# Every engine's work in another order: one table of dates replaced in a one-core kernel of three transformer blocks

## The reference

```python
hid = jnp.einsum('cd,ced->ce', xc, jnp.take(u, ec, axis=0))
w = gc * jax.nn.gelu(hid, approximate=False)
return jnp.einsum('ce,ced->cd', w, jnp.take(v, ec, axis=0))
```

## Time and profile before

| | us |
|---|---|
| median of three runs | 2318.24 |
| lowest and highest | 2311.13, 2322.93 |
| span of the profiled execution | 2204.1 |
| median less that span | 114.1 |

### The profile page before, as it was taken

One profiled execution on the slowest core, in us unless ns is written; L12 is line 12 of the kernel. 1 busy time (PEld: TensorE's weight loads), 2 busy tenths in 40 slices (PEclk: granted clock), 3 DMA queues, 4 the chain that ended last, 5 costly groups with the idle time before them and its releaser, 6 DMA issues.

```text
span 2204.1 us, 28240 instructions
## 1 busy us (share of the span) xinstructions
PE 1852.7 (84%) x10240; PEld 1223.7 (56%) x10240; DVE 1473.0 (67%) x3734; ACT 726.2 (33%) x1882; POOL 1124.4 (51%) x1028
## 2 busy tenths in 40 slices
PE   6999886689897687898677999877299988999998
PEld 3798575457544173545125565431166655567786
DVE  1388688855658776457896356587868778567564
ACT  3466123345422111321021153102025533346363
POOL 0000035575767676677776577676775667640000
PEclk8999897798898899999898999988689999999999
DMA  9999868799999999999999999999999999995360
GB/s 391 376 407 362 318 250 307 268 385 363 407 379 337 406 363 406 395 373 406 389 405 409 399 397 375 406 368 389 366 394 401 363 374 360 356 409 201 134 243 26
DMA packets 213459, 774.85 MB, mean 352 GB/s; under 512 B 23868, under 2 KB 24776, under 8 KB 213320
## 3 DMA queue, kind: packets, MB, share of 16 engines
q0 software_dynamic: 147456, 536.94, 63.5%
q1 hardware_dynamic: 65864, 236.11, 27.4%
HBM read 770.80 MB, written 2.16 MB: 351 GB/s over the span
## 4 chain that ended last, share of the span: by engine, by line
PE 39%; POOL 20%; DMA 18%; DVE 13%; issue 7%; ACT 2%; SPq 0%; DVEq 0%; ACTq 0%; POOLq 0%
POOL gat L1475 20%; PE ps L717 15%; DMA gat<-in_peer_v_dram,idxv 8%; DMA gat<-in_peer_u_dram,idx 7%; PE ps L1582 5%; DVE gat L1494 4%; PE ps L1235 3%; PE ps L1650 2%; PE ps L1013 2%; PE ps L1033 2%; PE ps L2723 1%; DVE ws L2108 1%; DVE ws L2106 1%; PE ps L821 1%; DMA wbuf<-in_win_dram 1%
## 5 line engine op out<-in xcount | busy, mean ns | idle before, releaser
L1494 DVE CUSTOM_DVE_ANT_0 gat<-gat,X 128x1024 f32<-128x1024 f32 x512 | 615.3, 1222 | 311.3 <-DMA gat<-in_peer_u_dram,idx 306.6
L1475 POOL DMA_INDIRECT gat<-in_peer_u_dram,idx x512 | 571.0, 1115 | 470.0 <-DVE ws L1327 292.2
L1475 POOL DMA_INDIRECT gat<-in_peer_v_dram,idxv x512 | 553.2, 1080 | 388.0 <-PE ps L1582 198.9
L717 PE MATMUL ps<-hn,wbuf 128*128 128x256 f32 (+1 forms) x2976 | 593.5, 357 | 38.6 <-DVE ws L1152 10.9
L717 PEld LDWEIGHTS ps<-hn,wbuf 128*128 128x128 f32 x2976 | 505.2, 197 | 124.6 <-issue 40.5
L1582 PE MATMUL ps<-gat,spread 128*32 128x512 f32 x2048 | 426.9, 656 | 113.0 <-DMA gat<-in_peer_v_dram,idxv 98.6
L1582 PEld LDWEIGHTS ps<-gat,spread 128*32 128x32 f32 x2048 | 81.8, 115 | 381.9 <-DMA gat<-in_peer_v_dram,idxv 227.8
L1235 PE MATMUL ps<-wbuf,oT 128*128 128x512 f32 x208 | 94.7, 609 | 2.7 <-DVE oT L1211 2.3
L1102 ACT ACTIVATE ws<-ws 128x16 f32<-128x16 f32 (+6 forms) x224 | 77.2, 347 | 35.0 <-DVE ws L1169 28.8
L861 DVE CUSTOM_DVE_ANT_0 gat<-gat,row 128x1024 f32<-128x1024 f32 x64 | 76.1, 1219 | 8.4 <-DMA gat<-in_ada_dram 4.3
L717 PE MATMUL ps<-ws,wbuf 128*128 128x256 f32 x256 | 61.9, 407 | 15.3 <-DVE ws L960 15.3
(11 more groups left out here) (373 smaller groups left out, 2599.1 us busy)
## 6 DMA issues: line engine op xcount, KB each, us to landing
wbuf<-in_win_dram SPq DMA_DIRECT2D x160, 512.0 KB, 8.3
gat<-in_ada_dram SPq DMA_DIRECT2D x120, 512.0 KB, 12.4
wbuf<-in_wout_dram SPq DMA_DIRECT2D x34, 512.0 KB, 6.5
wbuf<-in_pq_dram SPq DMA_DIRECT2D x32, 512.0 KB, 8.5
wbuf<-in_kvw_dram SPq DMA_DIRECT2D x32, 512.0 KB, 8.7
gat<-in_kvada_dram SPq DMA_DIRECT2D x16, 512.0 KB, 14.4
gat<-in_peer_u_dram,idx POOLq DMA_INDIRECT x512, 7.5
gat<-in_peer_v_dram,idxv POOLq DMA_INDIRECT x512, 7.8
```

The source lines that it names most:

```text
L717: i = e.do.matmul(psum, wview(name, g, kc // 2, turn)[:, kc % 2, m * P:m * P + P], src[:, kc, :], start=kc == 0, stop=kc == KC - 1)
L1475: e.do.indirect_dma_start(gat[g][:, :], None, t["peer_" + kind], bass.IndirectOffsetOnAxis(at, 0)).then_inc(*ldg[g].put(kind, l, b, *unit))
L1494: e.do.tensor_tensor_reduce(g[:, :], g[:, :], X[b % 2][:, :], 1.0, 0.0, ALU.mult, ALU.add, hid[:, e_ // 16 % 2, e_ % 16:e_ % 16 + 1]).then ...
```

## The change

The table `LATE` of corrections becomes a table `PLAN` of dates, now for all five engines, GpSimd too; where `PLAN` has a date, the base date no longer counts. The order in which weight tiles are loaded, and with it their slots, comes from a new list `LOADS`. No step has other instructions than before. Since waits are on semaphores' counts at the producer's place in its list, they move with the steps.

```diff
-def weave(late, *parts):
+def weave(at, *parts):
...
-        return t + late[n][step] if n < len(late) and step < len(late[n]) else t
+        return at[n][step] if n < len(at) and step < len(at[n]) else t
...
-    LATE = [
...
+    LOADS = [
+        ("win", 0, 0), ("win", 1, 0), ("win", 2, 0), ("win", 3, 0), ("win", 4, 0), ("win", 5, 0), ("win", 6, 0), ("win", 7, 0), ("wout", 0, 0),
...
+    PLAN = {
+        "PE": [
+            [6.57, 6.58, 11.07, 35.42, 38.1, 52.76, 53.2, 89.46, 93.11, 95.57, 104.82, 105.26, 118.16, 120.62, 129.86, 137.43],
...
-        loads.extend(sorted((when, key) for key, when in first.items()))
+        loads.extend(sorted(((when, key) for key, when in first.items()),
+                            key=lambda load: (LOADS.index((*load[1][:2], load[1][3])), load)))
...
-        weave(LATE_SP, *parts, sp_start(e), sp_ada(e), sp_weights(e), sp_kept(e), sp_sub(e), sp_bias(e), sp_store(e))
+        weave(PLAN["SP"], *parts, sp_start(e), sp_ada(e), sp_weights(e), sp_kept(e), sp_sub(e), sp_bias(e), sp_store(e))
...
-        weave([], *[pool_experts(e, l, c) for l in range(2) for c in range(2)])
+        weave(PLAN["POOL"], *[pool_experts(e, l, c) for l in range(2) for c in range(2)])
```

More of the change, by code:

```diff
@@ L446, in layer_stack_kernel @@
     T_FINISH = [1705.451, 1757.451, 1903.422, 2011.985]
-    LATE = [
-        [
[63 rows of a table removed]
-        ],
-        [
[68 rows of a table removed]
-        ],
-        [
[68 rows of a table removed]
-        ],
-        [
[3 rows of a table removed]
-        ],
-    ]
-    LATE_PE, LATE_ACT, LATE_DVE, LATE_SP = LATE
+    LOADS = [
+        ("win", 0, 0), ("win", 1, 0), ("win", 2, 0), ("win", 3, 0), ("win", 4, 0), ("win", 5, 0), ("win", 6, 0), ("win", 7, 0), ("wout", 0, 0),
+        ("wout", 1, 0), ("pq0", 0, 0), ("pq0", 1, 0), ("win", 1, 1), ("win", 0, 1), ("win", 2, 1), ("win", 3, 1), ("win", 4, 1), ("win", 5, 1),
+        ("win", 6, 1), ("win", 7, 1), ("wout", 0, 1), ("wout", 1, 1), ("pq0", 0, 1), ("pq0", 1, 1), ("sbq", 0, 0), ("sbq", 1, 0), ("kvw", 0, 0),
+        ("kvw", 2, 0), ("kvw", 1, 0), ("kvw", 3, 0), ("sbo", 0, 0), ("sbo", 1, 0), ("pq1", 0, 0), ("sbq", 0, 1), ("pq1", 1, 0), ("sbq", 1, 1),
+        ("kvw", 0, 1), ("kvw", 2, 1), ("kvw", 1, 1), ("kvw", 3, 1), ("sbo", 1, 1), ("sbo", 0, 1), ("pq1", 0, 1), ("pq1", 1, 1), ("win2", 7, 0),
[4 rows of a table added]
+    ]
+    PLAN = {
[69 rows of a table added]
+        ],
+        "ACT": [
[73 rows of a table added]
+        ],
+        "DVE": [
[70 rows of a table added]
+        ],
[5 rows of a table added]
+        ],
+        "POOL": [
[4 rows of a table added]
+        ],
+    }
     def t_sel(l, b, hh):
@@ L2882, in run_tensor @@
                     parts += [pe_choice(e, b, T_CHOICE[b])]
-        weave(LATE_PE, *parts)
+        weave(PLAN["PE"], *parts)
     def run_scalar(e):
@@ L2910, in run_scalar @@
                     parts += [act_choice(e, b, T_CHOICE[b])]
-        weave(LATE_ACT, *parts)
+        weave(PLAN["ACT"], *parts)
     def run_vector(e):
@@ L2934, in run_vector @@
                 parts += [dve_choice(e, b, T_CHOICE[b])]
-        weave(LATE_DVE, *parts)
+        weave(PLAN["DVE"], *parts)
     for run in (run_tensor, run_sync, run_gpsimd, run_scalar, run_vector):
```

## The result

| | median us | lowest to highest | ratio to before, 95% interval |
|---|---|---|---|
| before, 20 runs | 2316.6 | 2300.12 to 2335.13 | |
| changed, 20 runs | 2337.84 | 2319.91 to 2360.83 | 1.0083 (1.006 to 1.0106) |

What follows compares the result with a forecast made beforehand. DMA was taken as the bound from 420 to 1560 us and TensorE from 2001 us on. Terms +6 - 15 + 12 - 59 + 11 = -45 us took 2318.24 to 2273 us, range 2248 to 2304.

Steps and rivals of the forecast that it cites:

- The 114.1 us: Time around the profiled span of 2204.1 us, taken as unchanged to turn span 2159 into time 2273.
- Start, +6: Up to the first gather: seven weight tiles ahead of adaptive tiles cost 9 us, TensorE wins back 3.
- Hole, -15: 300 to 420 us, DMA share 0.80: earlier dots free GpSimd's tiles, winning some 0.6 of 24 us.
- The sign that I named: From 300 to 420 us, a DMA share of 0.9 or more would show the forecast right.
- From 420 to 1560 us, nothing: Middle stretch: DMA share 1.00 at 388 GB/s taken as the bound, so the sum had no term here.
- More tiles, +12: Before the last gather: twelve more weight tiles cost 16 us of DMA, of which idle share takes 4.
- the 55 us, +11: Before 2001 us: TensorE work moved out of the tail must fit there, delaying the end by 11 us.
- Tail, -59: From 2001 us to the end: 55 us of TensorE work leaves, 59 us at density 0.93.
- a fixed 19: Time from the end of the gathers to the last addition of expert sums, 19 us in the forecast's formula.
- Given back at the gathers: Rival, chance 0.09: each of the last 31 groups loses 1.2 us more, 37 us gone, 2310, no difference.
- late indices: Rival, chance 0.04: choice of experts for blocks 2 and 3 comes late; 110 us delay gives +26, 2344.
- The DMA rate: Rival, chance 0.04: from 300 to 1985 us, 370 instead of 388 GB/s gives +37, 2355.

Runs made afterwards that it cites:

- one hybrid: The change's order up to 285 us, the order of before from there: 2218.41 us, ratio 1.0019 to the kernel before.
- another: The order of before up to 285 us, the change's order from there: 2234.68 us, ratio 1.0083 to the kernel before.

## Why the prediction was wrong

- **The base.** The 114.1 us were no time around the span but the difference between two executions, perhaps on two chips. It spoils the number 2273, not its sign.
- **Start, +6.** The first gather was 14 us later (294.4, now 308.5). The first of VectorE's shifts, before and now:

```profile
L842 DVE TENSOR_TENSOR mod<-ps,vec x3: 170/173/176, 41.3 to 107.3; 128x16 f32<-128x16 f32 x3
```

```profile
L872 DVE TENSOR_TENSOR mod<-ps,vec x3: 167/174/176, 52.7 to 148.3; 128x16 f32<-128x16 f32 x3
```

It comes 11 us later, near my 9; the 3 us that I let TensorE win back are not there, 3 more were lost on the way. SyncE's waits from 40 to 120 us, of the changed kernel, then of before; L740 and L710 issue the weight tiles, L801 and L771 the adaptive ones:

```profile
SPq L740 <- PE ps L747: 31.2, 12, 14.8
SPq L801 <- PE ps L851: 28.9, 7, 7.9
```

```profile
SPq L771 <- PE ps L821: 46.3, 9, 9.8
SPq L771 <- DVE mod L861: 9.5, 5, 2.6
SPq L710 <- PE ps L717: 5.2, 8, 1.9
```

SyncE waits some 60 us in both, now in front of weight tiles, before in front of adaptive ones. From 60 to 80 us DMA's share is 0.62 where it was 1.02. In the end the start was worth 4 us by one hybrid and 8 by another, neither clear of its interval; the rest is won back in the first group.
- **Hole, -15.** Right in effect, and in the wait that it named: the first group is 14 us shorter, its 65th gather starts 118 us after the first instead of 141, and its stalls for dots fell from 39 to 7 us; 13.5 of these came back as one wait for index rows at 391 us. The sign that I named was wrong: DMA's share from 300 to 420 is 0.78, with TensorE's part of the work moved out of the stretch.
- **From 420 to 1560 us, nothing.** This is the step that failed. "The 1024 gathers and the weight tiles beside them are the bound, and TensorE and VectorE have room", I wrote from a share of 1.00 at 388 GB/s, and gave the stretch no term, though every list was re-ordered in it. The second and third group took 14 and 34 us more, 48 of the 80 us between my -45 and the +35, and without them that sum would come out faster, at -13. Two hybrids bear it out: these two groups alone in the change's order make the kernel 2.3% slower, and left in before's order, with the change's first group and end, it is 0.8% faster. What ran there in place of a DMA floor is the ring: GpSimd issues, and stands until TensorE has used a tile. A full share there was a result of well-placed lists, not a floor: with a sixth of the bytes away the time fell by 2% only.
- **More tiles, +12, and the 55 us, +11.** The fourth group took 29 us more; I had 23. Forty tiles were issued behind the last gather, as forecast.
- **Tail, -59.** From the last expert addition (2007.9, now 2080.1) to the end it is 203.2 and now 165.9 us, -37; TensorE's busy share in it is 149.03 of 165, 0.90 against 0.92. Another 6 us fell between the last gather and that addition (17.8, now 12.0), which I had taken as a fixed 19. The busy time that left is 186.4 - 149.0 = 37 us and not 55: the loss is in my estimate of what leaves, not in the density. I priced it line by line, and lines overlap: behind the last group the busy times of all lines add up to some 220 us where TensorE is busy 189, now to 169 for 151. By lines 51.5 us left, near my 55.
- **Rivals.** "Given back at the gathers" (0.09) was nearest, in its place and mechanism, but I priced it in the last 31 groups alone (37 us; 29 came there, 23 of them mine already) and not in the 62 before. Of late indices nothing shows at the places named (740, 1140, 1540 us); the one wait of 13.5 us for index rows is at 391. The DMA rate for a full share fell little: the two middle groups moved 377 GB/s at 0.99 and 364 at 0.97, which is 381 and 375, against 387 and 388. What part of the loss that is, no run shows. A chance of 0.82 for faster rested on one regime being DMA's alone.

## What to carry to other kernels

Where a ring of buffers feeds a queue that almost never catches up, count the stalls of that queue (gap less its least gap) by stage: they add up to the end, while a share of 1.00 of DMA, or one long wait of TensorE, says little of what a re-ordering is worth. Moving consumers earlier in an in-order list isn't safe either; here all three such moves cost time, and the wait went from one engine to another. And where a wait is removed, look at the engine's busy time in the stretch: twice here the wait went and the idle time stayed. When a new order is made of parts that can be separated, price each by a hybrid: here two parts were worth 0.8% together and two others cost more.

## What was not expected

- One edit of dates by 5 or 6 us in one engine's list costs 2.1% (before) and 3.3% (the changed kernel), more than the whole change.
- The changed kernel's instructions take the same times in both sessions (dots 1.22 us on average, the matmuls of expert groups 0.68 and 0.66), yet its span is 2328.2 in one and 2246.0 in the other. The stalls account for most of it: 128, 99, 121 and 156 us, 76 of the 82 us more. What makes them longer there stays open; the gathers' packets took 61.9% of 2328.2 us and 63.2% of 2246.0, 1.5% more in the slower one.
- The Trainium skill (DMA: Bandwidth & Descriptors, Anatomy of one DMA — SWDGE (gpsimd) path) gives 2.0 us plus the bytes over 436 GB/s for one transfer, an estimate of 3.2 us for a gather. Here the least is 4.1 and the median 7.5 us, with up to ten others in flight; the ring has to be sized by the second.
- Open is also which steps of the new lists make TensorE later at the tiles of the second and third group (in the third by 2.6 us behind the landing). It isn't the norm's 43.9 us alone; no single step was found.
